# A 256-token network in one kernel: output chunks loaded two turns behind, and the row-mean power between two low splits

## What is computed

```
# layer 0, latent attention (8 heads)
cq  = rms_norm(x @ w_dq) ; q = cq @ w_uq ; kv = rms_norm(x @ w_dkv) @ w_ukv
o_h = softmax((q_nope k_nope' + q_rope k_rope') * scale) @ v_h
x  += rms_norm(concat(o_h) @ w_o)
# layer 1, differential attention (8 heads)
a_h = softmax(q1 k1' * s - slope*dist) - lam * softmax(q2 k2' * s - slope*dist)
o_h = rms_norm(a_h @ v_h) * gain * (1 - lam_init)
x  += rms_norm(concat(o_h) @ w_o)
# last layer, output: merged = sigmoid(x@g_a)*(o_a@w_a) + sigmoid(x@g_b)*(o_b@w_b) ; merged @ w_out
```

## Time and profile before

| what | value |
|---|---|
| median of 3 runs | 1235.72 us (1234.78 to 1236.96) |
| profiled execution, its own time | 1238.13 us |
| its span | 1236.3 us |
| PE busy | 1105.7 us (89%) |
| DVE, ACT, POOL busy | 701.2, 562.7, 428.4 us |
| chain that ended last | PE 70%, DVE 12%, issue 9%, ACT 4%, POOL 3%, DMA 1% |
| DMA | 160.30 MB, mean 130 GB/s |

### The profile page before, as it was taken

One profiled execution on the slowest core, in us unless ns is written; L12 is line 12 of the kernel. 1 busy time (PEld: TensorE's weight loads), 2 busy tenths in 40 slices (PEclk: granted clock), 3 DMA queues, 4 the chain that ended last, 5 costly groups with the idle time before them and its releaser, 6 DMA issues.

```text
span 1236.3 us, 21016 instructions
## 1 busy us (share of the span) xinstructions
PE 1105.7 (89%) x7744; PEld 1024.5 (83%) x7744; DVE 701.2 (57%) x1048; ACT 562.7 (46%) x1007; POOL 428.4 (35%) x292
## 2 busy tenths in 40 slices
PE   6699899999999995999999886979797779969996
PEld 6689589999879884799999686979797679969996
DVE  3355577667666555576666626666565355543433
ACT  4344455555455554555555443333331045544442
POOL 0000133333412331234334527455444055533331
PEclk9899899999999998999999978989898989989998
DMA  8133265555433431455555203313131034444551
GB/s 300 60 98 129 84 221 194 180 186 183 137 123 119 136 134 57 150 188 186 181 177 184 105 18 119 102 36 103 35 102 52 1 120 153 136 136 135 193 183 51
DMA packets 45246, 160.30 MB, mean 130 GB/s; under 512 B 5136, under 2 KB 5392, under 8 KB 45072
## 3 DMA queue, kind: packets, MB, share of 16 engines
q1 hardware_dynamic: 44480, 157.06, 38.0%
q0 software_dynamic: 720, 2.62, 0.6%
HBM read 158.62 MB, written 1.05 MB: 129 GB/s over the span
## 4 chain that ended last, share of the span: by engine, by line
PE 70%; DVE 12%; issue 9%; ACT 4%; POOL 3%; DMA 1%; POOLq 0%; SPq 0%; DVEq 0%; ACTq 0%
PE work L370 12%; PE work L371 12%; PE work L372 12%; PE acc L370 6%; PE acc L371 6%; PE acc L372 6%; PE work L1329 5%; PE acc L1555 2%; PE acc L1563 2%; DVE silu L1372 1%; POOL low L342 1%; DVE conv L1365 1%; PE acc L1562 1%; DVE low L342 1%; ACT high L335 1%
## 5 line engine op out<-in xcount | busy, mean ns | idle before, releaser
L342 DVE TENSOR_TENSOR low<-raw,high 128x1024 fp32r<-128x1024 f32 (+2 forms) x191 | 282.0, 1485 | 193.5 <-ACT high L335 192.4
L342 POOL TENSOR_TENSOR low<-raw,high 128x1024 fp32r<-128x1024 f32 x110 | 267.5, 2435 | 306.9 <-ACT high L335 306.8
L335 ACT ACTIVATE high<-raw 128x1024 fp32r<-128x1024 f32 (+4 forms) x301 | 305.9, 1027 | 47.8 <-DMA raw<-in_w_out 23.9
L370 PE MATMUL work<-xh,high 128*128 128x256 f32 x1080 | 306.3, 284 | 4.4 <-POOL oal L2026 1.8
L371 PE MATMUL work<-xl,high 128*128 128x256 f32 x1080 | 303.5, 281 | 0.0
L372 PE MATMUL work<-xh,low 128*128 128x256 f32 x1080 | 303.3, 281 | 0.0
L370 PEld LDWEIGHTS work<-xh,high 128*128 128x128 f32 x1080 | 204.3, 189 | 9.5 <-issue 3.5
L371 PEld LDWEIGHTS work<-xl,high 128*128 128x128 f32 x1080 | 204.1, 189 | 1.9
L372 PEld LDWEIGHTS work<-xh,low 128*128 128x128 f32 x1080 | 204.1, 189 | 0.0
L918 POOL TENSOR_TENSOR h<-gelu,cv 128x256 f32<-128x256 f32 x44 | 49.8, 1131 | 202.0 <-ACT gelu L851 114.0
L1329 PE MATMUL work<-xh,high 128*128 128x256 f32 x256 | 79.2, 309 | 0.4 <-POOL low L342 0.3
(11 more groups left out here) (342 smaller groups left out, 2328.0 us busy)
## 6 DMA issues: line engine op xcount, KB each, us to landing
raw<-in_w_ffn SPq DMA_DIRECT2D x132, 512.0 KB, 4.2
raw<-in_w_out SPq DMA_DIRECT2D x40, 512.0 KB, 4.0
raw<-in_w_diff SPq DMA_DIRECT2D x32, 512.0 KB, 5.0
raw<-in_w_att SPq DMA_DIRECT2D x32, 512.0 KB, 4.1
raw<-in_w_gdn SPq DMA_DIRECT2D x24, 512.0 KB, 3.6
raw<-in_w_mla SPq DMA_DIRECT2D x8, 512.0 KB, 3.3
raw<-in_w_gdnz SPq DMA_DIRECT2D x8, 512.0 KB, 4.4
raw<-in_w_mla SPq DMA_DIRECT2D x8, 384.0 KB, 3.1
```

The source lines that it names most:

```text
L335: act.activation(high[k][:, 0:w], raw[k][:, 0:w], ACT.Copy).then_inc(high_done[k], 1)
L342: eng.tensor_tensor(low[k][:, 0:w], raw[k][:, 0:w], high[k][:, 0:w], ALU.subtract).then_inc(low_done[k], 1)
L370: pe.matmul(out, lhs[0], rhs[0], start=start, stop=False)
```

## The change

1. `Phase` gets a number `lag`, 1 by default. It is 2 for the latent (`mla`) and the differential phase (`diff`), whose lagging slots are 2 and 3, the output rows.
2. With lag 2, SP loads chunk 2 of the other slots ahead of its loop; in turn i the loop loads chunk i of these and chunk i-2 of the lagging slot (before: i-1). Chunk 6 of the lagging slot follows behind the loop, before the first chunks of the next phase; chunk 7 stays last.
3. The place of the lagging slot in a turn goes by the lag (before: by the number of turns being 8). So the output stage, with 8 turns and lag 1, now loads slot 4 behind slots 0 and 1 instead of last.
4. On GpSimd, in the differential phase, the root of head h is taken in head h between its two low splits (before: at the start of head h+1, behind both).

```diff
-        mla=Phase("mla", {0: MLA_QB * 256, 1: MLA_KVB * 256, 2: 1024}, HEADS, lagging=(2,)),
+        mla=Phase("mla", {0: MLA_QB * 256, 1: MLA_KVB * 256, 2: 1024}, HEADS, lagging=(2,), lag=2),
-        diff=Phase("diff", {k: 1024 for k in (2, 0, 1, 3)}, HEADS, (1, 3), (3,)),
+        diff=Phase("diff", {k: 1024 for k in (2, 0, 1, 3)}, HEADS, (1, 3), (3,), 2),
...
         def head(i):
             first = isinstance(i, int) and i == 0
             more = not (isinstance(i, int) and i == HEADS - 1)
-            if not first:
-                result_root(i - 1)
             if not more:
                 first_of_next(split, ph["diff"])
             if more:
                 refill(split, ph["diff"], 2, i + 1)
                 refill(split, ph["diff"], 0, i + 1)
                 refill(split, ph["diff"], 1, i + 1)
+            result_root(i)
             if not first:
                 refill(split, ph["diff"], 3, i - 1)
...
         over(pool, HEADS, head, 2)
-        result_root(HEADS - 1)
...
             for k in prompt:
                 load(sp, p, k, 1)
-            with sp.Fori(2, p.count) as r:
+            if p.lag == 2:
+                for k in prompt:
+                    load(sp, p, k, 2)
+            with sp.Fori(p.lag + 1, p.count) as r:
                 i = sp.snap(r)
 
-                order = [*prompt, *p.lagging] if late else [*prompt[:2], *p.lagging, *prompt[2:]]
+                order = [*prompt, *p.lagging] if p.lag == 2 else [*prompt[:2], *p.lagging, *prompt[2:]]
                 for k in order:
-                    load(sp, p, k, i - 1 if k in p.lagging else i)
+                    load(sp, p, k, i - p.lag if k in p.lagging else i)
+
+            if p.lag == 2:
+                for k in p.lagging:
+                    load(sp, p, k, p.count - 2)
             if p.lagging and late:
                 load_next(p, True)
```

More of the change, by code:

```diff
@@ L46, with __init__ @@
 class Phase:
-    def __init__(self, name, widths, count, gpsimd_low=(), lagging=()):
+    def __init__(self, name, widths, count, gpsimd_low=(), lagging=(), lag=1):
         self.name, self.widths, self.count, self.gpsimd_low, self.lagging = name, widths, count, gpsimd_low, lagging
+        self.lag = lag
         self.base = {}
```

## The result

The changed kernel takes **1249.29 us** (median of 4 runs, 1248.35 to 1251.39), the kernel before, beside it, 1235.95 us (4 runs). The ratio is 1.011, with a 95% interval of 1.0094 to 1.0126: slower by 1.1%. The profiled execution took 1251.39 us with a span of 1249.6, against 1238.13 and 1236.3 before, so 13.3 us more. The mean granted clock went from 0.955 to 0.946.

The account below looks back on a forecast made before the run. PE was taken as the bound: busy 50.5 of 50.7 us in latent attention, 15.1 of 16.1 in a differential head. Differential -4.8, latent +12.2, output 0 gave +7.4 us on the 1235.72 median: 1243.1 us, range 1236.5 to 1252.5.

Parts of the forecast that it names:

- Latent, +12.2: Latent heads 1 to 5: output chunk loaded too late for the running head, 5 x 2.45 = +12.2 us.
- landing at 92.47, ACT 2.62 us late: Latent head at 84 to 93: slot 2 lands 4.6 us after issue, while ACT wants it at 89.85.
- 2.45 us late: Latent heads: the late chunk delays DVE's qr_t, so PE's next scores start 2.45 us late in each head.
- rival C: Latent heads: PE gaps of 2.2 us drop the clock to 1.2 GHz, about 3 us each, 1253 us; chance 0.15.
- Differential, -4.8: Differential attention: sum of heads 3 to 5, head 6, head 7 and after head 7, -2.7 + 0.8 - 1.3 - 1.6.
- give back their whole 2.7 us: Differential heads 3 to 5: the root between the splits ends PE's wait for onorm, -2.7 us.
- +0.8, gains nothing: Differential head 6: second split, output chunk 6 and next layer's chunks come 0.8 us later, net +0.8 us.
- Head 7: "-1.3": Differential head 7: root ahead of the output split makes the mean short, so the softmax PE awaits comes earlier, -1.3 us.
- After head 7: -1.6, held by the low split: After differential head 7: onorm comes 1.7 us sooner, but the last output split holds the output product to 491.4, -1.6 us.
- Output stage, 0: Output stage: the new load order ends ACT's 23.9 us of DMA waits, but PE waits for none of it, value 0.
- Rival A: Differential attention: GpSimd's second split holds DVE's onorm, so the 4.8 us are lost, 1249.3 us; chance 0.10.
- Rival B: Latent heads: the output chunk lands within 2.4 us, in time, leaving only the differential gain, 1230.9 us; chance 0.08.

Follow-up runs that it names:

- e6: The whole change plus two filler products on TensorE in each latent head but the last, ahead of its wait for the transposed probabilities: 1245.77 us, ratio 1.0090 to before.
- e3: The kernel before with only the differential root moved between GpSimd's two low splits, all loads as before: 1236.69 us, ratio 1.0004.
- e4: The kernel before with only the differential output chunks loaded two turns behind, the root still behind both low splits: 1229.75 us, ratio 0.9955.
- e5: The kernel before with only chunk 4's place in the output stage's load queue changed: 1238.14 us, ratio 1.0012.
- e7: The whole change with the latent output chunk issued second of a turn's three loads instead of third: 1240.01 us, ratio 1.0033 to before.
- e9: The change without its latent part, next layer's first chunks before differential output chunk 6, 18 filler products in the last differential head: 1226.55 us, ratio 0.9920 to before.

## Why the prediction was right, and where its sizes were off

The direction, the place and the chain came out as written. The sizes of three terms did not, and one of the prediction's own signs of being wrong appeared: matmuls at half speed between 65 and 125 us. Two of the misses pulled against each other, which is luck: with the latent attention and the last layer as measured and the differential term as forecast the sum is +16.5, some 1252 us, just inside the range's upper end.

**Latent, +12.2: the mechanism right, one term of it missing.** The step "landing at 92.47, ACT 2.62 us late" measured 2.52 a head (12.6 over five). The landing of 4.6, taken from one row of head 0, is 4.7 as the median of the five chunks that stood third. The Trainium skill's page DMA: Bandwidth & Descriptors gives the formula that the prediction quotes (Anatomy of one DMA) for DMAs issued by GpSimd; these loads are issued by SP, so their 4.6 us are no test of it. "2.45 us late" for the next scores measured 2.5 to 2.6 where the clock was held (e6). Heads 1 to 5, with 6 and 7 nearly as before, is what the periods show. What failed is that this sum left the clock out: it stood as rival C with a chance of 0.15, and it came in four of five heads at about 1.8 us each, so 7.2 us, not the 3 us for each fall that C reckoned. So rival C, the forecast's late chunk with the clock on top, is what happened in the latent attention. The argument against it, "between them run some 9 us of dense matmuls", weighed too much. Behind gaps of 1.8 to 2.3 us the lower level followed in four cases of five, whatever dense work stood around them.

**Differential, -4.8: measured -8.0.**
- Heads 3 to 5: "give back their whole 2.7 us". They gave 3.8, and h1 and h2 another 0.24. The sum of waits undercounts: each of these heads is 1.2 to 1.3 us shorter where its wait was 0.9 on average. The step that failed is that the root's place gives this time back, with "they reached PE nowhere in heads 3 to 5" for the DMA waits. Either half of the change ends these waits (e3, e4), but only the early loads shorten the heads, and the root alone lengthens them. So the late loads did reach TensorE, by way of late splits and the root behind them.
- Head 6: "+0.8, gains nothing". It gave 1.1 in this execution. The step that failed is that everything there "starts 0.8 us later now", together with the value 0 for the early loads. With those loads GpSimd's first split starts 1.4 us ahead of the scores (466.60, scores at 468.05) and no longer with them, which is more than the 0.8 us that the root takes from the second split. e3, which has the root without the loads, shows what the step described: 19.26 us for head 6 and a loss in each head from the second on. The loads were "covered" for the kernel before, but not for the kernel with the root moved.
- Head 7: "-1.3". The softmax moved by 1.34. "After head 7: -1.6, held by the low split" measured 1.7 of the 2.85, with the wait of 1.23 us at 504.87 on just that split.

**Output stage, 0:** e5 has it at 0.12% with an interval across none. The +1.2 of the last layer lies within what it varies by from execution to execution.

**Rival A** is refuted: onorm started at 412.48 right behind prob, with GpSimd's split running from 410.76 to 413.16, and took 0.61 us. The rule of the Trainium skill quoted there (GPSIMD Engine Reference, Key points) fits: onorm was not held. That the total of 1249.3 hit the measured number is chance: A's sum lacks the differential gain, the measured one has it and the clock. **Rival B** is refuted by ScalarE's waits.

The sum by measured terms is +12.5 for lateness, +7.2 for the clock, +0.4 ahead of the first head, -8.0, and +1.2: 13.3 us. The forecast of +7.4 missed 7.9 on the latent side and 3.2 the other way.

## What to carry to other kernels

Before a load is set back a turn, write down for which head the engines split each chunk in the turn whose semaphores the queue waits on: the same lag was right in the attention that splits two heads ahead and wrong in the one that splits one ahead. When a step is moved behind a resource in a closed loop (split, buffer free, reload, next split), compare its cost with the slack of the loop and not with that at its own consumer: e3 removed the very wait it aimed at, its heads grew by 1.1 to 1.5 us, and nothing was gained by the medians. And price a new TensorE gap of about 2 us at nearly twice its length (here 10.1 us of gaps cost 19.7), and try whether a few products of filler, fitted by their measured duration, hold the clock.

## What the runs showed of the hardware that was not expected

- The granted clock fell to its lower level behind gaps of 1.8 to 2.3 us inside otherwise dense work (four of five heads), and held behind gaps of 0.6 to 1.1 us (e7). The length of the gap doesn't decide it alone: behind the same waits of 1.2 and 0.69 us in the last latent head it fell in six of twelve executions without filler there and held in the other six. Filler products held it: 1.00 over 24 us in e9.
- One and the same stretch of code, the latent attention, took 134.5 to 135.3 us in some executions and 138.1 to 138.3 in others, by whether its first head ran at full clock and whether its final product did. The runs of before scatter from 1230.5 to 1241.2 us, so gains of a few us are read from head periods, where these repeat, rather than from totals.
- A filler product of 128 x 512 in f32 took 0.88 us at full clock, and its two records start half of that apart; a row's count of instructions has to be divided by the records of one product before it is used as a price.
- A 512 KB chunk landed 3.1 to 3.3 us after its issue by itself, 3.7 to 5.1 as second of three loads and 4.3 to 4.8 as third (five chunks each, in before, e7 and the changed kernel).
